# A hybrid decoder block on one core: 26 unread TensorE products between the table of items and the first gathered tokens

## What is computed

```python
logits = (h @ router_w) + router_b
top_logit, top_idx = lax.top_k(logits, TOP_K)          # TOP_K = 4
gates = softmax(top_logit)
...
gu = xb @ w_gate_up[e] + b_gate_up[e]                   # xb: the tokens of one expert
gate, up = jnp.split(gu, 2, axis=-1)
gate = jnp.minimum(gate, 7.0)
up = jnp.clip(up, -7.0, 7.0)
act = (up + 1.0) * (gate * jax.nn.sigmoid(1.702 * gate))
y = act @ w_down[e] + b_down[e]
out[token] += y * gates[token, e]
```

## Time and profile before

| | |
|---|---|
| median of 3 runs | 2383.89 us |
| the three runs | 2383.89, 2376.93, 2384.17 us |
| the profiled execution | 2379.72 us, span 2378.0 us |
| TensorE busy | 2180.5 us, 92% of the span |
| VectorE, ScalarE, GpSimd busy | 1559.7, 1337.9, 329.5 us |
| mean granted TensorE clock | 0.961 |
| DMA | 536.95 MB, mean 226 GB/s |

### The profile page before, as it was taken

The page is one execution under the profiler, slowest core; times in us unless marked ns, Lnnn a source line. Parts: engine busy times, 40 slices in busy tenths (PEclk is TensorE's granted clock), DMA queues, the critical chain, the costliest instruction groups (busy, mean ns, idle before and its releaser), DMA issues.

```text
span 2378.0 us, 34508 instructions
## 1 busy us (share of the span) xinstructions
PE 2180.5 (92%) x10770; PEld 1800.4 (76%) x10771; DVE 1559.7 (66%) x1640; ACT 1337.9 (56%) x1523; POOL 329.5 (14%) x306
## 2 busy tenths in 40 slices
PE   6999878789389999998999999999999999999993
PEld 5889645589268887877887777778888887888873
DVE  4321256645548757767866988887666888667754
ACT  5111147723347546557765777776555777555654
POOL 1000000002312002111211112121120122122100
PEclk8999978999589999999999999999999999999997
DMA  5111300044369669869977999998777899777954
GB/s 189 54 53 36 106 1 1 5 182 108 109 239 321 227 198 306 299 228 330 361 268 244 361 370 356 372 362 286 227 229 231 304 367 361 231 232 241 306 167 161
DMA packets 265290, 536.95 MB, mean 226 GB/s; under 512 B 14479, under 2 KB 31145, under 8 KB 265133
## 3 DMA queue, kind: packets, MB, share of 16 engines
q1 hardware_dynamic: 248332, 488.26, 58.6%
q0 software_dynamic: 16896, 47.83, 8.4%
HBM read 499.29 MB, written 36.75 MB: 225 GB/s over the span
## 4 chain that ended last, share of the span: by engine, by line
PE 67%; issue 8%; DVE 7%; ACT 3%; DMA 1%; POOL 0%; DVEq 0%; ACTq 0%; SPq 0%; POOLq 0%
PE ps L672 63%; PE ps L889 1%; ACT hT_hi L1127 1%; PE ps L896 1%; DVE work L1383 1%; PE ps L812 1%; DVE hT_lo L1541 1%; DVE w_lo L1530 1%; ACT region_mem L1162 0%; DVE work L1581 0%; DVE hT_lo L1551 0%; ACT hT_lo L1175 0%; DVE weight_ring L1657 0%; PE ps L855 0%; DVE slots_between L1530 0%
## 5 line engine op out<-in xcount | busy, mean ns | idle before, releaser
L672 PE MATMUL ps<-hT_hi,hT_lo 128*128 128x512 f32 (+1 forms) x4304 | 1398.7, 389 | 12.4 <-DVE hT_lo L1551 12.3
L672 PEld LDWEIGHTS ps<-hT_hi,hT_lo 128*128 128x128 f32 x4304 | 808.3, 189 | 183.1 <-DVE w_lo L1530 18.2
L1127 ACT ACTIVATE hT_hi<-weight_ring 128x2048 fp32r<-128x2048 f32 x417 | 787.0, 1914 | 196.3 <-PE ps L672 142.5
L1530 DVE TENSOR_TENSOR slots_between<-weight_ring,hT_hi 128x2048 fp32r<-128x2048 f32 x245 | 552.9, 2286 | 141.2 <-ACT hT_hi L1127 138.9
L672 PE MATMUL ps<-slots_between,hT_lo 128*128 128x512 f32 x1344 | 527.0, 392 | 0.0
L1530 DVE TENSOR_TENSOR w_lo<-weight_ring,hT_hi 128x2048 fp32r<-128x2048 f32 x140 | 319.7, 2284 | 33.7 <-ACT hT_hi L1127 33.7
L672 PE MATMUL ps<-w_lo,hT_lo 128*128 128x512 f32 (+1 forms) x896 | 336.2, 375 | 0.0
L672 PEld LDWEIGHTS ps<-slots_between,hT_lo 128*128 128x128 f32 x1344 | 254.1, 189 | 54.2
L672 PEld LDWEIGHTS ps<-w_lo,hT_lo 128*128 128x128 f32 x896 | 168.7, 188 | 30.5
L590 POOL DMA_INDIRECT residual_rows<-work,idx_now x48 | 120.1, 2503 | 476.5 <-ACT work L1188 289.9
L672 PE MATMUL ps<-mem_there,picked 128*128 128x512 f32 x288 | 124.0, 431 | 28.1 <-issue 27.5
(11 more groups left out here) (251 smaller groups left out, 2470.2 us busy)
## 6 DMA issues: line engine op xcount, KB each, us to landing
weight_ring<-in_w_gate_up SPq DMA_DIRECT2D x280, 1024.0 KB, 7.8
weight_ring<-in_w_down SPq DMA_DIRECT2D x140, 1024.0 KB, 5.4
weight_ring<-in_w_mix_in SPq DMA_DIRECT2D x10, 1024.0 KB, 8.5
weight_ring<-in_x SPq DMA_DIRECT2D x8, 512.0 KB, 8.7
weight_ring<-in_w_mix_out SPq DMA_DIRECT2D x4, 1024.0 KB, 5.3
work<-in_x SPq DMA_DIRECT2D x8, 512.0 KB, 5.4
residual_rows<-work SPq DMA_DIRECT2D x8, 512.0 KB
normed_rows<-work SPq DMA_DIRECT2D x8, 512.0 KB, 5.2
```

Source lines behind the costliest of these rows:

```text
L672: return pe.matmul(o, l, r, start=first, stop=last)
L1127: act.activation(w_high_part(u), ring[:, home(u), :], ACT.Copy).then_inc(s["w_high_made"], 1)
L1530: dve.tensor_tensor(w_low_part(u), ring[:, home(u), :], w_high_part(u).bitcast(f32), ALU.subtract)\
```

## The change

TensorE makes 26 products after the wait for the table and before the wait for the first gathered block. Each takes the first 128 columns of `h2T` as the stationary and the 512 columns of its second half as the moving operand, both plain f32, and writes all of bank 3 of PSUM, as first and last of its sum. Nobody reads the bank before the items overwrite it.

```diff
@@ -961,6 +961,9 @@
                 for u in range(10, SLOTS):
                     use_unit(it, u, kinds)
 
+
+            for n in range(26):
+                mm(ps[:, 3, :], h2T[:, 0, :], h2T[:, 4:8, :].rearrange("p k t -> p (k t)"), True, True)
             for b in range(BLOCKS):
                 pe.wait_ge(s_gather[b], 16)
                 if b > 0:
```

## The result

The changed kernel takes 2387.73 us, median of 8 runs (2385.27 to 2392.17). The kernel before, run beside it, takes 2378.30, median of 8 (2372.72 to 2384.17; the three runs shown earlier are among them and happened to be high, their median 2383.89). The ratio is 1.0042 with a 95% interval of 1.0028 to 1.0057: about 10 us slower (7 to 14), just over what the prediction called the least difference that can be told. The profiled execution took 2391.07 us, span 2389.5, against 2379.72 and 2378.0: +11.4.

The account below looks back on a forecast made before the run. TensorE was taken to bound the kernel from the first item's first product on. 9.2 (products past the hole) - 2.1 (turnings) - 2.8 (idle time) = +4.3 us, on the three-run median, gave 2388 us; range 2380 to 2397.

Parts of the forecast that it names:

- My case: Products overrun the hole ahead of the first item: +4.3 us, spanning 2386 to 2392 us; chance 0.56.
- rival 2: At TensorE's jumps to and from the item's bodies, code fetches get dearer: 2391 to 2397 us, named 2393; chance 0.28.
- the loop: From the first item's first product on, a delay of that product moves the end by as much, nothing more.
- products past the hole: first turning later by: Before the first turning, products fill 24.7 us against a hole of 15.5 us, delaying that turning: +9.2 us.
- the two turnings at full clock: Both turnings of gathered tokens find a full clock, each 0.87 us in place of 1.94: -2.1 us.
- idle time ahead of the item (9.1): Between second turning and first product, code arrives sooner behind the weights, 3.5 us in place of 6.3: -2.8 us.
- cast to first product in all: From the table's copy to the item's first product: 9.2 - 2.1 - 2.8 = +4.3 us.
- The price of a product: Each added product is two passes, 0.854 us at full clock, 1.71 at half; 26 take 24.7 us.
- rival 1: The turnings keep the clock up until the first item, saving 2.3 us: sum +2.0, 2386 us; chance 0.07.
- The first jump: TensorE's jump to the first item's body waits for code behind 4 MB of weights; 3.5 us taken instead of 6.3.
- The check I named: TensorE's idle time behind 666 us should be 39.8 - 9.1 = 31 us within 2, else a step is wrong.
- Rivals 1, 3 and 4: 3: clock never rises for plain f32, 2410 us, chance 0.04; 4: products fit the hole, at best 2379.5, chance 0.05.

Follow-up runs that it names:

- e9: 14 of the plain f32 products and 72 tiny bf16 ones in the hole, added to the kernel before; 2359.31 us, ratio 0.9914.
- e10: e2 with SP's last four weight loads of item 0 held until TensorE has used its first unit; 2355.40 us, ratio 0.9898 against the kernel before.
- e3: 14 of the plain f32 products and 24 tiny bf16 ones in the hole, added to the kernel before; 2378.05 us, ratio 0.9997.
- e1: 52 tiny bf16 products (128x32) in place of the change's 26, same 104 instructions; 2381.48 us, ratio 1.0011 against the kernel before.
- e5: 86 tiny bf16 products in the hole and 7 plain f32 ones behind the second turning, added to the kernel before; 2359.52 us, ratio 0.9916.
- e8: 72 tiny bf16 products (144 instructions) in the hole, added to the kernel before; 2366.80 us, ratio 0.9944.
- e7: 81 tiny bf16 products (162 instructions) in the hole, added to the kernel before; 2410.78 us, ratio 1.0133.
- e2: 100 tiny bf16 products (200 instructions) in the hole, added to the kernel before; 2358.62 us, ratio 0.9917.
- e6: 100 small transposes (200 instructions) at the start of TensorE's program, none near the table, added to the kernel before; 2366.46 us, ratio 0.9942.
- e11: e9 with SP's last four weight loads of item 0 held until TensorE has used its first unit; 2357.00 us, ratio 0.9900 against the kernel before.

## Why the prediction was right and wrong

The time was named within 0.3 us of the median, and was in the range. That flatters it twice: it went from +4.3 us over a median of three that stood 5.6 us above that of the eight, and the true step is some 10 us. So the time was hit by luck: two errors of 5 us, one in the start and one in the step, cancelled. My case, "a loss too small to be told", was not what happened. In kind what happened is rival 2, which had 0.28, a new stall in the loop, and which I had put at 4.3 + 2.8 + 2.2 = 9.3; in size both terms were too small, the products (4.3, measured 6 to 7) and the loop (0, measured 7.4 in the trace and, as what is left, 2 to 3 in the medians). Step by step, from the cast of the table (in this way the 2.1 us of chance ahead of it drop out):

| step | forecast | in the trace |
|---|---|---|
| products past the hole: first turning later by | +9.2 | +9.5 (cast to turning 15.6, now 25.1) |
| the two turnings at full clock | -2.1 | -0.9 to the second's start, -0.5 in the second |
| idle time ahead of the item (9.1) | -2.8 | -2.0 |
| cast to first product in all | +4.3 | +6.1 (31.2, now 37.3) |
| the loop | 0 | +7.4 to the last item's last bias product |

- **The price of a product** held: 0.85 us from pass to pass until 637.6 (1.01 for the first), then 0.43, the clock full from about 638; 25.2 us against 24.7. No row of before shows the 1.71 us a product at half clock that the sum uses: it is twice the 0.854 of full clock, my estimate. The trace after shows it, passes 0.85 apart at a granted clock of 0.50 over 632 to 636, 1.71 a product; the factors 1.9 and 2.2 of the nearest rows would have given 1.6 and 1.9.
- **The turnings** were worth 1.4 us, not 2.1: the clock stood at 0.69 over 660 to 664, so it fell about when the second began, with TensorE idle for 2.6 us between the two; in e9, with the same gap, it did not. I had shown such a fall (605 to 608) and used it only against rival 1.
- **The first jump** gave 2.0 us of idle time, forecast 2.8. Its cause was read rightly, as e10 shows. But the branch still cost 4.6 us, more than the 3.5 I took from the mean of the later ones. e3 and e9 show the same from the other side: turnings that were done earlier were met by a wait of 8.6 and 9.2 us.
- **The loop at nothing** is the step that failed. I wrote that whatever moves the first product moves the end by as much and priced the loop at 0. In the trace it cost 3.3 us up to the start of the second item and 1.7 in the half clock behind it, together 5.1 of the 7.4 us. The other 2.3 are the sum of changes at the stalls that both kernels have: +2.8 at the ninth item, where the wait is 6.2 us for 4.7 and the half clock lasts longer, +1.6 at the last, where the wait of 2.4 us is followed by a spell at half clock and that of 2.2 in before was not, and together -2.1 elsewhere, over half of it at the fifth. Only 0.4 of the 2.3 are unnamed waits (21.6 - 18.4 - 2.8), most of the rest is time at half clock. That these differ for the change's sake and not by chance is not shown; e1 has the same +1.6 at the last item. The mechanism stood in the text as rival 2, with the right number of instructions, and with the one sentence that should have set its chance: "the shift can as well remove one". With stalls at some items and none at most, their number could hardly be expected to stay the same; "no change in the loop" was the special case, and 0.56 for it was too much. What I lacked was the half-clock spell in the price: most stalls cost their wait and 1.5 to 2.7 us behind it.
- The check I named, 31 us for TensorE's idle time within 2, was meant without the wait ahead of the first product (39.8 - 9.1). Like for like it came out at 21.6 + 12.5 = 34.1. By my own words that was the sign of a wrong step, and it is the wrong step: 2.8 us of it are the new wait. The first product, at 669.50, lay within 667 to 673, and the idle time ahead of it at 7.1 against 6.3.
- Rivals 1, 3 and 4 are out by the rows: 0.50 in the window of the item's start, full clock for plain f32 at 638, 52 passes.

The products alone cost 6 to 7 us by two pairs of kernels (6.2 and 7.2), which agrees with the 6.1 us from cast to first product in the trace. The change of the code's position makes the rest, 2.2 in the medians of e1, where it is within the scatter, and 7.8 in its trace.

## What to carry to other kernels

When an edit adds or removes instructions ahead of a loop or branch that the engine takes at run time, compare it with a filler of the same number of instructions before believing any difference of a per cent: here the position of the code was worth from -21 to +33 us, several times the edit. Count the code packets in the page's queues before and after, and look for unnamed waits and long branch records at the jumps; if there are some, try a few positions, since two hundred idle instructions in a hole bought more than any other edit here. Filler meant to warm the clock cost 6 to 7 us where it outlasted its hole, and in this place it did not pay even where it fitted (e9) or reached up to the work that it was to warm (e5).

## What the runs showed of the hardware beyond that

- TensorE's jumps within this loop take 0.20 us in the median (L370, 35 of them) or some microseconds, up to 5.6 after and 7.6 with 81 tiny, according to how many instructions stand ahead of the loop (none over 0.22 us at L370 with 100 tiny) and, at least once, to the timing (4.58 us at the ninth item in e1, 0.62 in e3). The waits were 1.9 to 4.7 us in most places, 6.2 after at the ninth item, up to 6.8 in e8 and 10.5 in e7.
- 18 instructions made 44 us: 2366.80 and 2410.78.
- Most stalls are followed by a spell at half clock, 0.62 in 737 to 741 after, 0.67 in 733 to 737 with 52 tiny: 13 or 14 matmuls where there are 19. Not all: the waits of 2.20 us at 1051 and 2.17 at 2306 in before are not.
- 52 products of 32 columns in bf16 take 1.57 us; 100 transposes of 22 columns in f32 took 10.84.

Open: which packets are fetched again and when (my estimates came near the times of e2, e7 and e8 and missed the number or the places of the stalls in e7 and e8), what besides the position decides a stall, the two groups of runs of the kernel before, and why e5, e6, e9 and e11 lose time within the first item.
